# Gated delta mixer: the turn at each level by four transpositions of 64x128 tiles in place of eight 64x64 unit products

## The reference

```python
decay = jnp.exp(jnp.where(incl, gc[..., :, None] - gc[..., None, :], NEG))
kb = k * beta[..., None]
m = jnp.where(strict, jnp.einsum('bhnid,bhnjd->bhnij', kb, k) * decay, 0.0)
a = m + jnp.eye(cs, dtype=F32)
rhs = jnp.concatenate([v * beta[..., None], kb * jnp.exp(gc)[..., None]], axis=-1)
sol = lax.linalg.triangular_solve(a, rhs, left_side=True, lower=True, unit_diagonal=True)
```

## Time and profile before

| | us |
|---|---|
| median of three runs | 5355.47 |
| the profiled execution | 5347.87 |
| its span, first to last instruction | 5346.1 |
| TensorE (PE) matmuls busy | 4164.6 (78%) |
| VectorE (DVE) busy | 2130.8 (40%) |
| ScalarE (ACT) busy | 1379.8 (26%) |
| GpSimd (POOL) busy | 1235.1 (23%) |
| mean granted clock of TensorE | 0.876 |

### The profile page before, as it was taken

How to read it: one execution, slowest core, us unless ns; L and a number is a source line. 1 busy time by engine, 2 the same in 40 slices (tenths; PEclk the granted TensorE clock), 3 DMA queues, 4 the chain that set the end, 5 groups by cost and what they waited for, 6 DMA issues and landing times. The chain is left out here.

```text
span 5346.1 us, 86327 instructions
## 1 busy us (share of the span) xinstructions
PE 4164.6 (78%) x35834; PEld 3405.5 (64%) x35834; DVE 2130.8 (40%) x2630; ACT 1379.8 (26%) x1713; POOL 1235.1 (23%) x892
## 2 busy tenths in 40 slices
PE   2998958676767599999982998949657774999994
PEld 1887835454656488888871886835446653877773
DVE  6445424465442623232326224324464435232234
ACT  3112132233231421212114112132242223322221
POOL 0000520103420332322212000520104402433332
PEclk9999568788888799999996998569778987999997
DMA  3444010100000111101001333010100011111112
GB/s 133 163 153 165 1 53 1 35 3 32 4 20 24 71 36 33 38 28 42 29 24 72 115 128 127 1 54 0 35 32 3 4 38 55 56 47 44 46 47 79
DMA packets 59944, 277.03 MB, mean 52 GB/s; under 512 B 6672, under 2 KB 6928, under 8 KB 54544
## 3 DMA queue, kind: packets, MB, share of 16 engines
q1 hardware_dynamic: 43824, 191.42, 10.7%
q10 hardware_dynamic: 15840, 81.53, 4.2%
HBM read 215.00 MB, written 50.07 MB: 50 GB/s over the span
## 5 line engine op out<-in xcount | busy, mean ns | idle before, releaser
L459 PE MATMUL ps<-h_hi,wu_hi 128*128 128x512 f32 (+1 forms) x1760 | 483.7, 372 | 41.8 <-PEq L455 38.9
L459 PE MATMUL ps<-h_hi,wu_raw_rest 128*128 128x512 f32 (+1 forms) x1760 | 482.4, 372 | 0.0
L459 PE MATMUL ps<-h_whole_rest,wu_hi 128*128 128x512 f32 (+1 forms) x1760 | 481.8, 371 | 0.0
L3001 DVE SCALAR_TENSOR_TENSOR y<-ps,taps,y 128x1023 f32<-128x1023 f32 (+1 forms) x132 | 134.1, 1016 | 853.8 <-DVEq L2999 846.5
L3030 POOL TENSOR_TENSOR wu_raw_rest<-wu_raw,wu_hi 128x1024 fp32r<-128x1024 f32 x88 | 210.8, 2395 | 1038.2 <-POOLq L3029 1038.2
L459 PE MATMUL ps<-h_hi,w_hi 128*128 128x512 f32 x1296 | 327.0, 361 | 85.2 <-PEq L455 85.2
L459 PEld LDWEIGHTS ps<-h_hi,wu_hi 128*128 128x128 f32 x1760 | 308.7, 189 | 105.7 <-issue 47.4
L3022 DVE TENSOR_TENSOR xT<-ps,xT 128x1280 f32<-128x1280 f32 (+1 forms) x176 | 239.0, 1358 | 340.9 <-DVEq L3018 340.9
L459 PEld LDWEIGHTS ps<-h_hi,wu_raw_rest 128*128 128x128 f32 x1760 | 309.2, 189 | 59.3
L459 PEld LDWEIGHTS ps<-h_whole_rest,wu_hi 128*128 128x128 f32 x1760 | 308.9, 188 | 59.2
L459 PE MATMUL ps<-h_hi,w_raw_rest 128*128 128x512 f32 x1296 | 325.8, 360 | 0.0
(11 more groups left out here) (305 smaller groups left out, 7611.6 us busy)
## 6 DMA issues: line engine op xcount, KB each, us to landing
wu_raw<-in_w_up_dram SPq DMA_DIRECT2D x88, 512.0 KB, 3.6
rows<-rows ACTq DMA_DIRECT2D x54, 640.0 KB, 5.3
w_raw<-in_w_in_dram SPq DMA_DIRECT2D x54, 512.0 KB, 4.7
ada_w<-in_ada_rest_dram ACTq DMA_DIRECT2D x27, 1024.0 KB, 7.3
wd_raw<-in_w_down_dram SPq DMA_DIRECT2D x44, 512.0 KB, 4.2
raw<-rows SPq DMA_DIRECT2D x24, 640.0 KB, 4.3
ada_w<-in_ada_rest_dram ACTq DMA_DIRECT2D x27, 512.0 KB, 5.1
oT<-rows SPq DMA_DIRECT2D x20, 640.0 KB, 5.1
```

Source lines behind the costliest of these rows:

```text
L459: mm = pe.matmul(ps[:, lo:lo + width], w[a][:, t, :], rhs[b][:, t, lo:lo + width], start=(t == 0 and i == 0), stop=(t == n_k - 1 and i == 2))
L3001: dve.scalar_tensor_tensor(y[:, s, lo + 1:hi], ps[s][:, lo:hi - 1], k.taps[:, s, 0:1], y[:, s, lo + 1:hi], ALU.mult, ALU.add).then_inc(own ...
```

## The change

`value_and_turn` issues the turn of `Ti` differently. Before, eight matmuls per direction and level took one 64x64 matrix each as weights and the unit matrix as moving operand. Now four calls of `pe.transpose` take two neighbouring matrices (`2 * a` and `2 * a + 1`) as one weight tile of 64 partitions x 128 columns, with the same unit matrix as moving operand, and write all 128 partitions of the same 64 PSUM columns. What lies in PSUM afterwards is the same, and so are the semaphores.

```diff
--- before.py
+++ after.py
@@ -1523,10 +1523,11 @@
                             pe.matmul(L[d][half[p], at:at + HD], left[half[r], 2 * a + p, :],
                                       Ti[d][i % 2][half[r], 2 * a + p, :], start=True, stop=True)
                     for a in both:
-                        for p, r in quads:
+                        for r in both:
                             at = at_pair(r, a, 1)
-                            mm = pe.matmul(L[d][half[p], at:at + HD], Ti[d][i % 2][half[r], 2 * a + p, :], eye[half[r], :],
-                                           start=True, stop=True)
+                            mm = pe.transpose(L[d][:, at:at + HD],
+                                              Ti[d][i % 2][half[r], 2 * a:2 * a + 2, :].rearrange("q p f -> q (p f)"),
+                                              eye[half[r], :])
                     mm.then_inc(pair_done[d].sem, 1)
```

## The result

The changed kernel takes 5402.47 us (median of four runs, 5399.98 to 5407.99); the kernel before took 5356.3 us on the same chip (four runs). The ratio is 1.009, with a 95% interval of 1.0072 to 1.0107: **46 us slower**. The forecast was 5448 with a range of 5378 to 5525. The profiled execution of the changed kernel took 5401.28 us.

What follows compares the result with a forecast made beforehand. No engine is full; each mixer step is a chain between TensorE, ScalarE and VectorE. Sum: 5348 + 44 (shapes) - 11 (instruction waits) + 60 (clock) = 5441, plus 7.6 to the median, 5448 us; range 5378 to 5525.

Steps and rivals of the forecast that it cites:

- Rival (c): TensorE takes the 64x128 tile straight behind 64x64 tiles, so only lost instruction waits count: faster, 5333 to 5345 us; 6%.
- (e): In the turn, a transposition comes as two records or longer ones, runs of 0.65 us: 5450 to 5560 us; 5%.
- Rival (d): The array empties, but slack elsewhere in the chain or saved waits pay for it: no change, 5345 to 5366 us; 4%.
- The term for the shapes: TensorE's array empties between value products and turns at each tile shape change: 2.2 us a step, 20 steps, +44 us.
- T's run: One direction's turn on TensorE, four transpositions: 0.47 us from first start to last end, against 0.41 for the old products.
- the second copy: ScalarE's copy for the second direction in levels 3 to 5: starts 1.67 us after the first value product, +0.48 us each.
- the fill of level 1: TensorE lines directly behind the second turn in level 1: start at 1.53 us instead of 0.95, +0.58 us a step.
- The instruction waits: TensorE waits named "issue", read as running out of instructions, 9.5 us in the first stretch: about half go, -11 us.
- The clock: TensorE's low-clock share in the mixer stretches rises from 18% to half: +60 us, bounds nothing to +185.
- +3.0 a step: Mixer step going from 29.0 to 32.0 us with half of it at low clock, making +60 us.
- rival (a): The mixer's clock stays about as it is, low share up to 0.3: 5388 us, up to 5410; 20%.
- the likeliest band: Mixer low-clock share between 0.3 and 0.8: 5410 to 5517 us; 55%.

Runs made afterwards that it cites:

- e3: Kernel before with the turn as four ordinary f32 products with 64x128 weights per direction and level instead of transpositions: 5479.12 us, ratio 1.0264.
- e6: Kernel before with e2's needless products, plus two one-column products with 64x128 weights between value and turn of each group: 5399.7 us, ratio 1.0109.
- e1: Changed kernel plus a needless product with 128x128 weights behind the product of levels 2, 3 and 4, in TensorE's wait: 5317.76 us, ratio 0.9947.
- e2: Kernel before plus the same needless products with 128x128 weights at levels 2, 3 and 4: 5316.52 us, ratio 0.9949.
- e7: Changed kernel with 18 needless products with 64x64 weights at each of e1's places, bringing the record count nearly back: 5319.05 us, ratio 0.9954.
- e8: Changed kernel with the needless 128x128 product at level 3 only: 5339.06 us, ratio 0.9991.

## Why the prediction was right or wrong

**The direction was right, and so were the parts of the mechanism; their sizes were not.** The forecast was 93 us slower, measured are 46. Line 1528 has 800 records, as said:

```profile
L1528 PE MATMUL lv<-mix,Ti x800: 222/272/367, 1280.3 to 4343.9; 64*128 64x64 f32 x160
```

V1's last record ends at 1494.169 (start 1493.951 and 0.218 us) and T1, behind it, starts at 1494.10: 0.07 us before that end, the distance of the earlier trace rows. e3 and e6 show that it is the tile shape. Rival (c), that the array takes the tile straight behind the others, is out. So is (e): four records, 0.34 us. Rival (d), no change, is out by the two comparisons at 1.009; but its reason, that the saved waits pay for the shapes, is what e1 and e2 show once the clock is held.

**The term for the shapes was mis-sized: 44 us forecast, about 18 measured.** The cleanest full-clock steps are 25.95 us in e1 and 25.03 in e2: 0.92 a step where the prediction had 2.2; times 20 is 18. (The shorter steps early in the second layer, 24.53 and 23.59, differ by as much.) Three of its own steps were too long. T's run is 0.34 us, not 0.47: the four transpositions come in pairs 0.11 us apart, and the last record is 0.222 long where I had taken 0.25. T1 thus ends at 1.37 and not 1.60, the second copy starts at 1.41 and not 1.67 (1.19 before), the fill of level 1 at 1.31 and not 1.53 (0.95 before). And 3 x 0.22 + 0.36 + 0.2 would be 1.2 a step, so a quarter of what is late in a level is also taken up by slack further on.

**The instruction waits: -11 forecast, about -17 found.** (The prediction's own working, 2 x 9.5 / 2, gives 9.5 and not 11.) In the whole mixers the shape term is 18.4 us and at equal clock the change costs 1.1, which leaves -17.3. That is a remainder and not a measurement, but the count agrees: 18.9 us of such waits in e2 and none in e1. In the 18 intervals the remainder is -11.5 (5.1 less 16.6), the count 12.5 and none. The argument for it, 14% fewer instructions, was wrong, as e7 shows.

**The clock: half of a stretch was low, as forecast, but it cost 36 us and not 60.** The granted clock is 0.75 in both stretches, within the 0.7 to 0.8 named, and the price of 0.28 us per low microsecond, from the earlier trace rows, is close to the 0.25 and 0.26 of e8 and e1. What failed is the step "+3.0 a step", the difference of two prices: half of 32.0 us low at 0.28 (4.5) less 18% of a step at 0.28 (1.5). Measured, the changed kernel has 14.6 us low in a step of 29.2, since its steps are shorter by what the shapes cost less, and pays 3.8 (68.0 / 18); and the low time of the kernel before was dearer than priced, 1.9 a step (34.3 / 18, 0.41 per low us). That leaves 1.9 a step: 33.7 us in 18 intervals, 36.2 in the whole mixers. The full-clock step was also set too long: 25.95 us measured (e1) and not 27.5; a step with 17 us low took 30.7. And if the 10.7 us of waits that the filler took from the kernel before in these stretches are counted as waits, the clock's part is 44 us there and the waits' part -22; the traces don't fix that split. Why the clock fell from 0.91 to 0.75 was not shown by any run.

**Together:** 18.4 - 17.3 + 36.2 = 37.3 us, the growth of the two mixers in the profiled execution; the middle term is a remainder, so the sum has to come out. The medians have 46, and the difference lies outside the mixers and stays open. The time lies where rival (a) put it (5388 to 5410), yet (a) is not what happened: the clock did fall, to half. The range held the time because its lower end reached down to that case: luck as to the size, for the likeliest band began at 5410.

**The rule on transpositions and the clock** (the Trainium skill, "TensorE: Matmul & The Clock Gate", Part 4: a transposition does not count for the clock as a matmul does). By that rule the stretches should have run mostly low, 5520 to 5570. They ran half low, as in e3 with its ordinary products (0.72 and 0.75 against 0.75 and 0.75). So nothing here shows the transposition as such to be worse for the clock than a product in its place; e3 has longer steps as well, so it doesn't disprove the rule either.

## What to carry to other kernels

Count the changes of tile shape on TensorE before the instructions: here the fewer instructions gave back some 17 us of waits, and the changes of shape took some 18. Put groups of one shape next to each other (V0, T0, T1, V1 was 25 us better than V0, T0, V1, T1, about 10 of them with the clock held). Where a kernel is a chain of short bursts and the granted clock swings, measure the clock apart with a needless product in a wait; here that is also the improvement, 31 us for the kernel before and 36 with the new order. A gain or a loss that is read at a swinging clock can be mostly the clock's: 34 of the 39 us in these stretches.

## What the runs showed of the hardware

- A f32 transposition of a 64x128 tile with 64 columns is one record at full clock, 222 or 272 ns long, four in 0.34 us; a f32 product of the same shape is two records, four of them in 0.66 us.
- A group of another tile shape starts 0.07 us before the last record ahead of it ends. Four records of one column, which change the shape twice, moved the group behind them by 0.43 us (e6).
- The granted clock does not follow TensorE's busy time in the records: it fell from 0.91 to 0.75 while the matmuls' busy time in the first stretch rose from 184.2 to 222.5 us. One 128x128 product in each of three levels brought it to 1.00. What made it fall was not shown.
- Long bursts of four-quarter 64x64 products at 15 ns a record are broken by waits of 0.3 to 1.4 us at places that are multiples of 256 instructions apart, 29.3 us in the two mixers of the kernel before. They all but vanish when the bursts are shorter, also with as many records (e7).
